# Attention heads of the second block: split products for scores and suffix sums, the suffix product inside the fourth slot

## The reference

```python
def stick_breaking_attention(q, k, v):
    ...
    for start in range(0, S, BLOCK_Q):
        ...
        z = jnp.einsum('bhqd,bhkd->bhqk', qb, kb) * scale
        causal = s_idx < t_idx
        log_keep = jnp.where(causal, jax.nn.log_sigmoid(-z), 0.0)
        later = lax.cumsum(log_keep, axis=3, reverse=True) - log_keep
        weights = jnp.where(causal, jnp.exp(jax.nn.log_sigmoid(z) + later), 0.0)
        outs.append(jnp.einsum('bhqk,bhkd->bhqd', weights.astype(vb.dtype), vb))
    return jnp.concatenate(outs, axis=2)
```

## Time and profile before

| | us |
|---|---|
| median of 3 runs | 3511.78 (3511.09 to 3512.23) |
| the profiled execution, whole | 3503.65 |
| its span, first to last instruction | 3501.8 |
| TensorE busy | 3374.8 (96%) |
| VectorE busy | 1766.1 (50%) |
| ScalarE busy | 1372.6 (39%) |
| mean granted TensorE clock | 0.989 of 2.4 GHz |

### The profile page before, as it was taken

The page is one execution under the profiler, slowest core; times in us unless marked ns, Lnnn a source line. Parts: engine busy times, 40 slices in busy tenths (PEclk is TensorE's granted clock), DMA queues, the critical chain, the costliest instruction groups (busy, mean ns, idle before and its releaser), DMA issues.

```text
span 3501.8 us, 51377 instructions
## 1 busy us (share of the span) xinstructions
PE 3374.8 (96%) x20948; PEld 2660.2 (76%) x20948; DVE 1766.1 (50%) x2313; ACT 1372.6 (39%) x1584; POOL 410.0 (12%) x718
## 2 busy tenths in 40 slices
PE   7899999999999999999999998999999999899897
PEld 1566888887887887887788876888888867677685
DVE  5745666665656433334323348242424237778545
ACT  1323344343334223334323227141414147777423
POOL 0000222322122000000000000000000014444000
PEclk9999999999999999999999999999999999999998
DMA  9522232323332442222232323333333333333322
GB/s 346 183 78 76 102 102 90 108 99 102 99 108 90 147 148 85 72 96 72 73 101 90 110 96 116 120 120 120 121 122 122 123 111 80 83 71 78 127 96 72
DMA packets 178956, 381.46 MB, mean 109 GB/s; under 512 B 111728, under 2 KB 117104, under 8 KB 145008
## 3 DMA queue, kind: packets, MB, share of 16 engines
q1 hardware_dynamic: 164352, 326.73, 28.5%
q0 software_dynamic: 14448, 52.50, 4.4%
HBM read 342.49 MB, written 35.13 MB: 108 GB/s over the span
## 4 chain that ended last, share of the span: by engine, by line
PE 86%; DVE 3%; DMA 3%; POOLq 3%; SPq 2%; issue 1%; ACT 1%; DVEq 0%; POOL 0%; ACTq 0%
PE PJ L291 19%; PE PJ L293 18%; PE PJ L292 18%; PE AB L291 6%; PE AB L293 6%; PE AB L292 6%; POOLq L1532 1%; POOLq L1529 1%; PE AB L230 1%; DMA WK<-ada 1%; DMA X<-blocks_scratch 1%; PE AB L658 1%; PE AB L1167 1%; PE AB L1627 1%; PE AB L440 1%
## 5 line engine op out<-in xcount | busy, mean ns | idle before, releaser
L291 PE MATMUL PJ<-XH,WH 128*128 128x512 f32 x2848 | 1131.9, 397 | 17.2 <-DVE XL L414 10.3
L293 PE MATMUL PJ<-XH,WL 128*128 128x512 f32 x2848 | 1112.3, 391 | 0.0
L292 PE MATMUL PJ<-XL,WH 128*128 128x512 f32 x2848 | 1111.4, 390 | 0.0
L322 DVE TENSOR_TENSOR WL<-RAW,WH 128x2048 fp32r<-128x2048 f32 (+2 forms) x239 | 545.0, 2281 | 658.7 <-ACT WH L317 653.3
L317 ACT ACTIVATE WH<-RAW 128x2048 fp32r<-128x2048 f32 (+2 forms) x240 | 453.4, 1889 | 848.5 <-PE PJ L293 589.2
L291 PEld LDWEIGHTS PJ<-XH,WH 128*128 128x128 f32 x2848 | 536.1, 188 | 144.0 <-issue 31.7
L293 PEld LDWEIGHTS PJ<-XH,WL 128*128 128x128 f32 x2848 | 535.7, 188 | 112.7
L292 PEld LDWEIGHTS PJ<-XL,WH 128*128 128x128 f32 x2848 | 536.4, 188 | 110.7 <-issue 3.8
L291 PE MATMUL AB<-XH,WH 128*128 128x512 f32 (+1 forms) x960 | 381.1, 397 | 10.2 <-DVE XL L414 7.7
L293 PE MATMUL AB<-XH,WL 128*128 128x512 f32 (+1 forms) x960 | 375.4, 391 | 0.0
L292 PE MATMUL AB<-XL,WH 128*128 128x512 f32 (+1 forms) x960 | 375.2, 391 | 0.0
(11 more groups left out here) (417 smaller groups left out, 3733.7 us busy)
## 6 DMA issues: line engine op xcount, KB each, us to landing
RAW<-w SPq DMA_DIRECT2D x232, 1024.0 KB, 4.9
WK<-ada SPq DMA_DIRECT2D x32, 1024.0 KB, 5.4
GATE<-gate POOLq DMA_DIRECT2D x64, 256.0 KB, 3.1
rkvg_scratch<-WK POOLq DMA_DIRECT2D x16, 1024.0 KB, 4.8
x_scratch<-X POOLq DMA_DIRECT2D x8, 1024.0 KB, 6.1
X<-rkvg_scratch SPq DMA_DIRECT2D x32, 256.0 KB, 3.5
RAW<-rkvg_scratch SPq DMA_DIRECT2D x32, 256.0 KB, 3.5
X<-xT SPq DMA_DIRECT2D x4, 1024.0 KB, 15.7
```

Source lines behind the costliest of these rows:

```text
L291: nc.tensor.matmul(bank[0:width, n, :], hi, xh, start=first, stop=False)
L292: nc.tensor.matmul(bank[0:width, n, :], hi, xl, start=False, stop=False)
L293: m = nc.tensor.matmul(bank[0:width, n, :], lo, xh, start=False, stop=last)
L322: nc.vector.tensor_tensor(WL[k % 2][:, :, 0:w], narrow(RAW[k % 2], w), WH[k % 2][:, :, 0:w].bitcast(F32), ALU.subtract).then_inc(wl_ready, 1)
```

## The change

The scores and the suffix product are made of high and low parts, as the projections are.

- Scores: `sb_act_pre` on ScalarE also copies q and k together (128x1024) to QK_HI in fp32r, and VectorE in step 0, ahead of v's copy, writes QK_LO = qk - QK_HI. TensorE makes three products for each of the four blocks: 12 matmuls in place of 4.
- Suffix product: the two constant matrices are copied to fp32r once at the program's start (MATR, they hold only 0 and -1). The softplus is split into SP_HI (ScalarE, 128x1280) and SP_LO (VectorE), the two sums into LATER_HI and LATER_LO (VectorE, two copies and two subtractions of 384 and 256 columns). TensorE makes two products in place of one for each: 14 matmuls in place of 7.
- Place: the suffix product moves from behind slot 2 to inside slot 3, behind column tile n = 1, by `between`.
- With `pull=True` the split for slot 3 is done in iteration 1, ahead of step 1, in place of iteration 2.

The product with v (step 3) stays fp32, and the steps of VectorE and ScalarE behind the suffix product stay as they are.

```diff
             for k in range(SLOTS):
-                if ahead - 1 <= k < SLOTS - 1:
+                if ahead - 1 <= k < SLOTS - 1 and not (pull and k == 2):
                     split(act, G, k + 1)
-                elif k == SLOTS - 1 and not last:
+                if pull and k == 1:
+                    split(act, G, 3)
+                if k == SLOTS - 1 and not last:
                     next_split(act, G + 1, 0)
                 if k < SLOTS - 1 and steps is not None:
                     steps(k)
```

`dve_group` is changed in the same way. The steps of ScalarE ahead of the group and of TensorE:

```diff
         def sb_act_pre(act, h, G):
...
             nc.scalar.activation(wk(16), wk(3), ACT.Silu).then_inc(sk("gs"), 1)
+            act.drain()
+            nc.scalar.activation(QK_HI, wk(0, 2), ACT.Copy).then_inc(sk("gs"), 1)
...
                 for kb in range(TB):
-                    m = nc.tensor.matmul(AB[:, kb, kb * P:SEQ], wk(1)[:, kb * P:(kb + 1) * P], wk(0)[:, kb * P:SEQ],
-                                         start=True, stop=True)
+                    at, z = slice(kb * P, (kb + 1) * P), AB[:, kb, kb * P:SEQ]
+                    nc.tensor.matmul(z, kh[:, at], qh[:, kb * P:], start=True, stop=False)
+                    nc.tensor.matmul(z, kh[:, at], ql[:, kb * P:], start=False, stop=False)
+                    m = nc.tensor.matmul(z, kl[:, at], qh[:, kb * P:], start=False, stop=True)
                 m.then_inc(sk("zt"), 1)
-            elif k == 2:
-                wait(pe, sk("sp"), h + 1)
+            elif k == "later":
+                wait(pe, sk("sp"), 2 * h + 2)
                 for kb in range(TB):
                     more = kb < TB - 1
-                    m = nc.tensor.matmul(AB[:, kb, kb * P:SEQ], mat("neg_suffix"), PK(10, kb), start=True,
-                                         stop=not more)
+                    z, at = AB[:, kb, kb * P:SEQ], slice(COL_O[kb], COL_O[kb] + COL_W[kb])
+                    nc.tensor.matmul(z, NEG_SUFFIX, SP_HI[:, at], start=True, stop=False)
+                    m = nc.tensor.matmul(z, NEG_SUFFIX, SP_LO[:, at], start=False, stop=not more)
                     if more:
-                        m = nc.tensor.matmul(AB[:, kb, (kb + 1) * P:SEQ], mat("neg_ones"), later_sum(kb),
-                                             start=False, stop=True)
+                        z = AB[:, kb, (kb + 1) * P:SEQ]
+                        nc.tensor.matmul(z, NEG_ONES, LATER_HI[kb], start=False, stop=False)
+                        m = nc.tensor.matmul(z, NEG_ONES, LATER_LO[kb], start=False, stop=True)
                 m.then_inc(sk("later"), 1)
```

ScalarE in step 1 (`sb_act`):

```diff
+                wait(act, sk("sp"), 2 * h + 1)
+                nc.scalar.activation(SP_HI, WK[:, 10 * SEQ:10 * SEQ + CAUSAL], ACT.Copy).then_inc(sk("log"), 1)
```

VectorE in step 0 (`sb_dve`):

```diff
                 wait(dve, sk("v_t"), h + 1)
+                wait(dve, sk("gs"), 2 * h + 2)
+                nc.vector.tensor_tensor(QK_LO, wk(0, 2), QK_HI.bitcast(F32), ALU.subtract)
                 nc.vector.tensor_copy(wk(15), AB[:, 0, :]).then_inc(sk("v"), 1)
```

VectorE in step 1:

```diff
-                dve.drain().then_inc(sk("sp"), 1)
+                dve.drain()
+                for kb in range(2):
+                    nc.vector.tensor_copy(LATER_HI[kb], later_sum(kb))
+                dve.drain()
+                for kb in range(2):
+                    nc.vector.tensor_tensor(LATER_LO[kb], later_sum(kb), LATER_HI[kb].bitcast(F32), ALU.subtract)
+                wait(dve, sk("log"), 2 * h + 2)
+                nc.vector.tensor_tensor(SP_LO, sp, SP_HI.bitcast(F32), ALU.subtract).then_inc(sk("sp"), 1)
```

TensorE's call of the groups, and the start of VectorE's program:

```diff
             with pe.Fori(1, HEADS) as h:
-                pe_group(pe, G_EVA + h, steps=lambda k: sb_pe(pe, h - 1, k))
+                pe_group(pe, G_EVA + h, steps=lambda k: sb_pe(pe, h - 1, k),
+                         between=lambda n, m: n == 1 and sb_pe(pe, h - 1, "later"))
...
             dve.wait_ge(consts_in, 48)
...
+            nc.vector.tensor_copy(NEG_SUFFIX, mat("neg_suffix"))
+            nc.vector.tensor_copy(NEG_ONES, mat("neg_ones"))
```

More of the change, by code:

```diff
@@ L135, in build @@
         RAW = [sb(f"RAW{r}", [P, SKT * GC]) for r in range(2)]
+        WK_AT = (2 * KT + 4 * SKT + KT + 2 * SKT) * SEQ
         NWK = 18
+        TBL_AT = WK_AT + NWK * SEQ
         WK = sb("WK", [P, NWK * SEQ])
@@ L149, in build @@
         GATE = [sb(f"GATE{r}", [P, SEQ]) for r in range(2)]
+        MATR = sb("MATR", [P, 2 * P], F32R)
         PJ = ctx.enter_context(nc.psum_tensor("PJ", [P, 4, SEQ], F32))
@@ L353, in act_group @@
         def act_group(act, G, evac, steps=None, pre=None, last=False, split=act_split, next_split=act_split, by_tile=False, early=False,
-                      ahead=2, split_first=False):
+                      ahead=2, split_first=False, pull=False):
             for k in range(SLOTS):
-                if ahead - 1 <= k < SLOTS - 1:
+                if ahead - 1 <= k < SLOTS - 1 and not (pull and k == 2):
                     split(act, G, k + 1)
-                elif k == SLOTS - 1 and not last:
+                if pull and k == 1:
+                    split(act, G, 3)
+                if k == SLOTS - 1 and not last:
                     next_split(act, G + 1, 0)
@@ L378, in dve_group @@
         def dve_group(dve, G, evac, steps=None, pre=None, last=False, split=dve_split, next_split=dve_split, by_tile=False, early=False,
-                      ahead=2, split_first=False):
+                      ahead=2, split_first=False, pull=False):
             for k in range(SLOTS):
-                if ahead - 1 <= k < SLOTS - 1:
+                if ahead - 1 <= k < SLOTS - 1 and not (pull and k == 2):
                     split(dve, G, k + 1)
-                elif k == SLOTS - 1 and not last:
+                if pull and k == 1:
+                    split(dve, G, 3)
+                if k == SLOTS - 1 and not last:
                     next_split(dve, G + 1, 0)
@@ L1146, in build @@
         BASE = 2 * HEADS
+        SPLIT_HI = placed("SPLIT_HI", [P, 3 * SEQ], TBL_AT + CAUSAL + SEQ)
+        SB_LO = placed("SB_LO", [P, 16 * SEQ], WK_AT)
+        QK_HI, QK_LO = SPLIT_HI[:, 0:2 * SEQ], SB_LO[:, 0:2 * SEQ]
+        SP_HI, SP_LO = SPLIT_HI[:, 0:CAUSAL], SB_LO[:, 10 * SEQ:10 * SEQ + CAUSAL]
+        LATER_HI = (SB_LO[:, 14 * SEQ + P:15 * SEQ], SPLIT_HI[:, CAUSAL:CAUSAL + 2 * P], SP_HI[:, COL_O[3]:CAUSAL])
+        LATER_LO = (SB_LO[:, 13 * SEQ:13 * SEQ + COL_W[1]], SB_LO[:, 13 * SEQ + COL_W[1]:13 * SEQ + COL_W[1] + COL_W[2]],
+                    SP_LO[:, COL_O[3]:CAUSAL])
+        NEG_SUFFIX, NEG_ONES = MATR[:, 0:P], MATR[:, P:2 * P]
         def sb_act_pre(act, h, G):
@@ L1158, in sb_pe @@
                 wait(pe, sk("v"), h + 1)
+                ql, kl = QK_LO[:, 0:SEQ], QK_LO[:, SEQ:2 * SEQ]
+                qh, kh = QK_HI[:, 0:SEQ], QK_HI[:, SEQ:2 * SEQ]
                 for kb in range(TB):
[L1160 to L1161 removed]
+                    at, z = slice(kb * P, (kb + 1) * P), AB[:, kb, kb * P:SEQ]
+                    nc.tensor.matmul(z, kh[:, at], qh[:, kb * P:], start=True, stop=False)
+                    nc.tensor.matmul(z, kh[:, at], ql[:, kb * P:], start=False, stop=False)
+                    m = nc.tensor.matmul(z, kl[:, at], qh[:, kb * P:], start=False, stop=True)
                 m.then_inc(sk("zt"), 1)
[L1163 to L1164 removed]
+            elif k == "later":
+                wait(pe, sk("sp"), 2 * h + 2)
                 for kb in range(TB):
                     more = kb < TB - 1
[L1167 to L1168 removed]
+                    z, at = AB[:, kb, kb * P:SEQ], slice(COL_O[kb], COL_O[kb] + COL_W[kb])
+                    nc.tensor.matmul(z, NEG_SUFFIX, SP_HI[:, at], start=True, stop=False)
+                    m = nc.tensor.matmul(z, NEG_SUFFIX, SP_LO[:, at], start=False, stop=not more)
                     if more:
[L1170 to L1171 removed]
+                        z = AB[:, kb, (kb + 1) * P:SEQ]
+                        nc.tensor.matmul(z, NEG_ONES, LATER_HI[kb], start=False, stop=False)
+                        m = nc.tensor.matmul(z, NEG_ONES, LATER_LO[kb], start=False, stop=True)
                 m.then_inc(sk("later"), 1)
@@ L1211, in sb_dve @@
                 nc.vector.scalar_tensor_tensor(a, z, -1.0, z, ALU.mult, ALU.max).then_inc(sk("abs"), 1)
-                wait(dve, sk("log"), h + 1)
+                wait(dve, sk("log"), 2 * h + 1)
                 nc.vector.scalar_tensor_tensor(sp, z, 0.0, a, ALU.max, ALU.add)
@@ L1218, in sb_dve @@
                     nc.vector.tensor_tensor(d, d, mat("later_only"), ALU.mult)
-                dve.drain()
+                dve.drain().then_inc(sk("sp"), 1)
                 nc.vector.tensor_tensor(later_sum(1)[:, P:2 * P], PK(10, 2)[:, P:2 * P], PK(10, 3), ALU.add)
@@ L1236, in sb_dve @@
                 wait(dve, sk("o"), h + 1)
-                wait(dve, sk("gs"), h + 1)
+                wait(dve, sk("gs"), 2 * h + 2)
                 wait(dve, s("res_stored"), 64)
@@ L2340, in _ @@
             with pe.Fori(1, HEADS) as h:
-                pe_group(pe, G_EVA + h, steps=lambda k: sb_pe(pe, h - 1, k))
```

(13 more changed lines are left out.)

## The result

The changed kernel took 3518.81 us (median of 7 runs, 3515.87 to 3522.56), the kernel before beside it 3509.98 us (7 runs, 3502.12 to 3512.23). The ratio is 1.0028 with a 95% interval of 1.0018 to 1.0038: the change costs 6 to 13 us. A second set of 12 runs gave 1.0026 (1.0015 to 1.0036). The median of the forecast was 3516.1, its range 3508 to 3527.

What follows compares the result with a forecast made beforehand. TensorE, busy throughout the stage, was taken as the bound. Base 3511.78 us, plus 3.9 for eight heads (2.24 wait less 1.75 saved each), plus 0.4 for copies at the start, gave 3516.1 us; range 3508 to 3527.

Steps and rivals of the forecast that it cites:

- The bound: Second block's eight projection groups: TensorE busy 52.00 of 52.00 us, so only matmul time or TensorE waits change the time.
- The matmul time: Scores from 2.16 to 1.90 us, suffix product from 3.56 to 2.07 us: 1.75 us saved per head.
- (b): Narrow split products in scores and suffix product cost fp32's price, 1.0 us saved per head: 3522 us, chance 0.15.
- (e): Narrow products in scores and suffix product with free weights, 3.31 us in all: 3511 us, chance 0.07.
- the 2.4 end: Bound on the new products' saving: no weight limit and no fixed part, 2.4 us saved per head.
- The wait: At each group's end TensorE stands 2.24 us per head, behind VectorE's queued split and copy of the finished bank.
- rival (a): At the group's end split and bank copy find cover, so the saving survives: 3498 us, chance 0.08.
- The clock: At restarts behind the eight waits the granted clock falls at two or fewer; chance 0.43.
- rival (c): Clock falls at restarts behind the waits: 3526 us at all eight, 3521 at half; chance 0.22 for four or more.
- What is hidden: New VectorE and ScalarE steps ahead of the suffix product, 3.6 us on VectorE, stay covered with 1.0 us left.
- rival (d): Suffix product waits for its operands: 3524 us if the new steps take 5.6 us, not 3.6; chance 0.05.
- The +0.4 us for the two copies at the start: Two 128x128 copies in VectorE's chain ahead of the first group cost 0 to 0.44 us, taken as 0.4.

Runs made afterwards that it cites:

- n = 0: The changed kernel with the suffix product behind the first column tile of slot 3 in place of the second: 3498.93 us, ratio 0.9974.
- the move alone: The changed kernel with the kernel before's fp32 products for scores and suffix sums, without high and low parts; move into slot 3 and pull remain: 3525.49 us, ratio 1.0043.

## Why the prediction was right, and where not

**The bound.** TensorE, with no wait in the stage: right. All that moved the time was matmul time and TensorE's waits, apart from the clock.

**The matmul time.** Predicted 1.90 and 2.07, measured 1.91 and 2.12. The saving of 1.75 per head is 1.69 by the two steps and 1.64 to 1.72 by whole groups. The price of the narrow products was the step with the least ground, and rows 5, from another stage, carried it: 128-column products start 0.11 us apart (1424.03 to 1424.14), 256-column ones 0.11 to 0.13 and 384-column ones 0.17. Rivals (b) and (e) fall. 128 columns at 2.4 GHz are 0.053 us, so something else than the columns sets the 0.11, and it is the time that rows 5 show for products of 64 columns with 128 weights. The weight loads of the new products last 187 to 189 ns, as those of fp32. The Trainium skill (TensorE: Matmul & The Clock Gate, Weight-path perf modes) has faster weight loads where there are 128 weights and the type is not FP32. These rows show no such gain for this kind. The forecast's price of that rule, 5 us, was too high by its own terms: without the limit of the weights it had 0.3 us per head, 2.5 us in all, and the 2.4 end needs the fixed part to go as well.

**The wait.** Predicted from R, where the stream resumes (now 1390.61 less a pitch, 1390.38): additions at +0.19, split done +8.31, copy done +9.48, at pace +9.85. Measured: +0.15, +8.26, +9.41, +9.74. So 2.13 us are lost, 2.24 were forecast. (In rival (a) the forecast's sum goes under 3504.8 when the wait falls below 0.83 us, not 0.9; nothing rests on it.) The restart is 0.33 behind the copy, not 0.37. Net without the clock 0.41 per head, 0.49 forecast.

**The clock.** This was the step that failed in the likeliest case. I let it stand for two falls or fewer and gave four or more a chance of 0.22, as rival (c); five came in both profiles of the changed kernel. The reasoning placed the wait between a stretch of 1.54 us that kept the clock and one of 2.57 that lost it, and gave the lower chance to the fall, without a row that says so. As shown idle it is 1.87. A fall costs 1.61 us, and not 1.2: eight matmuls lie at the lower level, not six. Rival (c) with five falls and this price is 3509.98 + 3.3 + 8.1 = 3521, against 3518.81 measured. That the sum came out 2.7 us from the median is partly luck: the forecast's own +4.3 us stand against +8.8 by the medians and +6 to +13 by the ratio's interval, and 1.8 us of the 4.5 that are missing were made up by the base, 3511.78 over 3 runs against 3509.98 over 7.

**What is hidden.** The operands of the suffix product were in time in the changed kernel, no wait ahead of L1189 (rival (d) falls). The cover was 1.67 us and not 1.0 (SP_LO ends at 1386.61, TensorE comes at 1388.28). The softplus chain is as forecast; the new steps took 2.93 us in place of 3.6. The copies into the split type take 0.36 and 0.29, not 0.51 and 0.36, the subtractions 0.56 and 0.42, a little more than forecast, and the rows overlap where the forecast had gaps. For n = 0 the expectation used the measured end of the operands and gave 1.0 to 1.2 of waiting; 0.94 was measured. The forecast's own numbers would have given 1.7. The +0.4 us for the two copies at the start is not seen: the first copy of the bank in the stage came 0.25 us earlier than before, not later.

**Chances.** "Slower" by more than 0.2% had 0.42, "same" 0.50. The medians are 0.25% apart, the ratio 1.0028 with its lower end at 1.0018; the interval holds 0.2% itself, so the runs leave open which of the two it was; both stood at near one half.

**Open.** What decides which of the waits of 1.87 us is followed by the lower clock: five of seven in both profiles of the changed kernel, three of seven waits of 1.9 in the move alone. It is hardly chance from one wait to the next, since both profiles of the changed kernel have it behind the same five. And what lowers the clock behind the stage, where the 2.7 us come from. Such differences come without a change: runs of the kernel before alone, in the sets of the experiments, lie between 3498.68 and 3516.59, and they go with the clock. Where its mean was 0.987 or more they took 3498.68 to 3506.96, where it was 0.983 or 0.984 they took 3507.45 to 3516.59.

## What to carry to other kernels

When a step that others wait for is moved later, list what stands in the queues behind the waiting instructions; here the result of the step itself was in time, and the split and the copy queued behind it were late. The split could have been done before the wait, as its earlier place shows, and the copy stood ready to start when the slot was done at about 1396. Work whose inputs are ready belongs ahead of the wait: one line on each of two engines turned 0.28% slower into 0.38% faster. That this holds up nobody has to be seen in the trace: here VectorE was still idle for 1.73 us behind the moved split. And a wait of TensorE can have a price above its length: here 2.13 us where the clock stayed and 3.7 where it fell.

## What the runs showed of the hardware

- In this stage the granted clock fell behind shown idle times of 1.87 us (five of seven), 1.9 (three of seven) and 2.8 us (seven of eight), and not behind 0.94, 1.5, 1.73 or 1.76. Each fall behind 1.87 us cost 1.61 us of stream. These are no bounds for other places: in the kernel before the clock was 0.50 from 3241.7 us, behind an idle time of 1.67, and in the kernel after 0.50 from 3146.2, behind one of 1.29 (both in stages with other short waits close by). The expectation from the kernel before, where 1.54 had kept it and 2.57 not, left this open.
- Eight products that nobody reads, put into the wait, kept the clock at 1.00 through the stage (0.98 without them), and the medians are 7.7 us apart.
- VectorE's copy from fp32 into the split type takes 0.36 us for 384 columns and 0.29 for 256, where its subtractions into this type take 0.56 and 0.42:

```profile
L1257 DVE TENSOR_TENSOR SB_LO<-WK,SB_LO 128x384 fp32r<-128x384 f32 x8 | 4.5, 558 | 0.6
...
L1254 DVE CAST SB_LO<-WK 128x384 fp32r<-128x384 f32 x8 | 2.9, 362 | 0.6
```
